# One-core transformer step on Trainium2: first modulation group loaded and multiplied in four parts, row vectors loaded later, overflow test moved before a wait

## The reference, cut to what matters

```
sh1, sc1, g1, sh2, sc2, g2 = split(silu(c) @ w_mod + b_mod, 6)      # w_mod: 1024 x 6144
h  = rmsnorm(x, norm1) * (1 + sc1) + sh1
p  = h @ w_in                                                       # 1024 x 1696, then three kinds of attention
x  = x + g1 * (heads_out @ w_out)
h2 = rmsnorm(x, norm2) * (1 + sc2) + sh2
x  = x + g2 * hier_moe(h2)                                          # 16 experts, each token goes to 2 of them
```

## Time and profile before

| | |
|---|---|
| median of three runs | 1391.71 us (1390.19 to 1394.88) |
| the profiled execution's own time | 1388.07 us |
| its span, first to last instruction | 1386.1 us |
| mean granted TensorE clock in it | 0.956 of full speed |
| PE busy | 1250.2 us, 90% |
| DVE, ACT, POOL busy | 539.7 us (39%), 377.7 us (27%), 156.2 us (11%) |
| DMA moved | 313.85 MB, mean 226 GB/s |
| SP's queue (q1), POOL's queue (q0), ACT's queue (q10) | 239.46, 47.20, 26.22 MB |

### The profile page before, as it was taken

One profiled execution on the slowest core, in us unless ns is written; L12 is line 12 of the kernel. 1 busy time (PEld: TensorE's weight loads), 2 busy tenths in 40 slices (PEclk: granted clock), 3 DMA queues, 4 the chain that ended last, 5 costly groups with the idle time before them and its releaser, 6 DMA issues.

```text
span 1386.1 us, 16841 instructions
## 1 busy us (share of the span) xinstructions
PE 1250.2 (90%) x5876; PEld 720.3 (52%) x5876; DVE 539.7 (39%) x1391; ACT 377.7 (27%) x963; POOL 156.2 (11%) x259
## 2 busy tenths in 40 slices
PE   3999989899999999999789997989999999999970
PEld 2455555565566554444355554556556655444430
DVE  0213256445565441121143324654546544111117
ACT  0112256434333111111012114653533311111111
POOL 3201120000000120000132003000000012000005
PEclk9999989998999999999989998999899999999995
DMA  9987577499111599999863047332001149999946
GB/s 336 393 293 253 199 278 268 147 360 331 41 61 62 203 336 384 359 373 365 299 239 105 22 167 265 123 123 68 32 31 62 61 191 333 397 369 368 366 167 227
DMA packets 125453, 313.85 MB, mean 226 GB/s; under 512 B 9841, under 2 KB 58257, under 8 KB 112705
## 3 DMA queue, kind: packets, MB, share of 16 engines
q1 hardware_dynamic: 90192, 239.46, 47.5%
q0 software_dynamic: 13136, 47.20, 9.1%
q10 hardware_dynamic: 22048, 26.22, 5.4%
HBM read 232.14 MB, written 80.71 MB: 226 GB/s over the span
## 4 chain that ended last, share of the span: by engine, by line
PE 81%; DVE 8%; issue 4%; ACT 3%; DMA 2%; POOL 1%; SPq 0%; DVEq 0%; ACTq 0%; POOLq 0%
PE ps L740 17%; PE ps L817 16%; PE ps L666 10%; PE ps L470 9%; PE ps L837 8%; PE ps L531 8%; PE ps L552 3%; PE ps L488 3%; DVE arena L1642 2%; PE ps L763 2%; PE ps L475 1%; DMA big<-in_x 1%; PE ps L606 1%; PE ps L517 1%; PE ps L781 1%
## 5 line engine op out<-in xcount | busy, mean ns | idle before, releaser
L740 PE MATMUL ps<-ring,big 128*128 128x384 f32 (+2 forms) x640 | 232.3, 522 | 3.9 <-ACT big L1196 3.9
L740 PEld LDWEIGHTS ps<-ring,big 128*128 128x128 f32 x640 | 121.0, 191 | 107.2 <-issue 64.7
L817 PE MATMUL ps<-ring,arena 128*128 128x512 f32 x384 | 169.3, 594 | 2.2 <-ACT arena L1289 2.0
L531 PE MATMUL ps<-arena 64*128 64x128 f32 (+5 forms) x576 | 143.4, 452 | 20.6 <-DVEq L1644 13.5
L470 PE MATMUL ps<-consts,arena 128*128 128x128 f32 (+2 forms) x872 | 130.2, 281 | 17.4 <-ACT arena L1112 6.2
L470 PEld LDWEIGHTS ps<-consts,arena 128*128 128x128 f32 (+2 forms) x872 | 103.7, 144 | 81.2 <-issue 53.6
L666 PE MATMUL ps<-ring,big 128*128 128x512 f32 x320 | 143.0, 598 | 0.9
L1112 ACT ACTIVATE arena<-ps 128x384 f32<-128x384 f32 (+3 forms) x140 | 69.0, 493 | 224.2 <-PE ps L470 223.7
L531 PEld LDWEIGHTS ps<-arena 64*128 64x128 f32 (+1 forms) x576 | 82.3, 208 | 80.8 <-issue 69.0
L817 PEld LDWEIGHTS ps<-ring,arena 128*128 128x128 f32 x384 | 71.2, 190 | 83.4 <-issue 83.4
L666 PEld LDWEIGHTS ps<-ring,big 128*128 128x128 f32 x320 | 59.0, 190 | 70.5 <-issue 66.4
(11 more groups left out here) (204 smaller groups left out, 1389.6 us busy)
## 6 DMA issues: line engine op xcount, KB each, us to landing
ring<-in_w_mod SPq DMA_DIRECT2D x40, 1024.0 KB, 10.6
ring<-in_w_up SPq DMA_DIRECT2D x22, 1024.0 KB, 9.3
ring<-in_w_gate SPq DMA_DIRECT2D x22, 1024.0 KB, 7.7
slots<-zeros ACTq DMA_DIRECT2D x8, 2560.0 KB, 18.7
slots<-zeros SPq DMA_DIRECT2D x8, 2560.0 KB, 20.3
arena<-in_w_down SPq DMA_DIRECT2D x16, 1024.0 KB, 13.0
slots<-arena POOLq DMA_DIRECT2D x32, 512.0 KB, 9.4
arena<-slots SPq DMA_DIRECT2D x30, 512.0 KB, 6.0
```

What stands on the lines that cost most here:

```text
L531: mm = pe.matmul(two(2 * h)[:, at:at + hi - lo], queries(pr, h), keys(pr, h, lo, hi), start=(at % 512 == 0), stop=True, skip_group_check=True)
L740: mm = pe.matmul(ps[:, c, 0:CHUNKS[c][1]], hT[:, s, k, :], slot[c][:, k, 0:CHUNKS[c][1]], start=(k == 0), stop=(k == KD - 1))
L817: mm = pe.matmul(ps[:, b, :], xgT[:, b, k * P:(k + 1) * P], w_gu[q][:, :, k, :], start=(k == 0), stop=(k == KD - 1))
```

## The change

1. *Norm weights in `consts`.* `n1c` and `n2c` become the columns behind the identity in `consts`. Their loads and semaphores go. `consts` comes in two loads: the first `HEAD` = 160 columns (identity and norm weights, 80 KB, semaphore `head_in`) and the rest (`const_in`).
2. *Group 0 in four parts.* Sixteen loads of 512 KB in place of eight of 1024 KB, with a semaphore for each pair of slices `k`. The order on SP's queue is now: part 0, tile 0's rows, part 1, the head of `consts`, part 2, part 3, chunk 0, tile 1, chunks 1 to 3, the rest of `consts`, tiles 2 to 4. PE multiplies a part when it is there; `turn_entry(0, 0)` comes after part 2; `spin(3, 6)` stands behind each of the parts 0, 1 and 2, in place of one `spin(3, 16)`; a `spin(3, 5)` stands behind `mod_columns(0)`.
3. *`cc` on ACT's queue* in place of SP's.
4. *`zero_fill` on ACT* one step later, at `s` = 1 to 4.
5. *`vector_loads(0)`* is issued by POOL after `entry(0, 1)` and the wait for the lane M, in front of the cache loads.
6. *DVE's wait for `const_in`* stands in front of the first rotary step and not at the start.
7. *Overflow test.* The load of the count and the branch come before the wait for the last stores; inside the branch the wait is repeated.

```diff
@@ tensor engine
-                    pe.wait_ge(mod0_in[ks[0] // 4], 64)
+                    pe.wait_ge(mod0_in[ks[0] // 2], 64)
...
-            mod_group(0, 0, range(0, 4))
-            pe.wait_ge(const_in, 16)
-            turn_entry(0, 0)
-            spin(3, 16)
-            mod_group(0, 0, range(4, 8))
+            for quarter in range(4):
+                mod_group(0, 0, range(2 * quarter, 2 * quarter + 2))
+                if quarter == 2:
+                    pe.wait_ge(head_in, 16)
+                    turn_entry(0, 0)
+                if quarter < 3:
+                    spin(3, 6)
             mod_columns(0)
+            spin(3, 5)
@@ sync engine
-            sp.dma_start(cc[:, 0, :], ...).then_inc(c_in, 16)
-            sp.dma_start(cc[:, 1, :], ...).then_inc(c_in, 16)
...
-            for half in range(2):
-                ks = slice(4 * half, 4 * half + 4)
+            for quarter in range(4):
+                ks = slice(2 * quarter, 2 * quarter + 2)
                 for i in range(4):
-                    sp.dma_start(slot0[i][:, ks, :], w_mod[:, ks, i * 512:(i + 1) * 512]).then_inc(mod0_in[half], 16)
-                if half == 0:
-                    sp.dma_start(consts[:, :], t_in["consts"]).then_inc(const_in, 16)
-                    sp.dma_start(n1c[:, :, :], t_in["norm1"]).then_inc(n1_in, 16)
-                    sp.dma_start(n2c[:, :, :], t_in["norm2c"]).then_inc(n2_in, 16)
+                    sp.dma_start(slot0[i][:, ks, :], w_mod[:, ks, i * 512:(i + 1) * 512]).then_inc(mod0_in[quarter], 16)
+                if quarter == 0:
                     x_load(t_in["x0"], 0)
+                if quarter == 1:
+                    sp.dma_start(consts[:, 0:HEAD], t_in["consts"][:, 0:HEAD]).then_inc(head_in, 16)
             in_load(0, 0)
             x_load(t_in["x0"], 1)
             in_load(0, 1)
             in_load(0, 2)
             in_load(0, 3)
+            sp.dma_start(consts[:, HEAD:], t_in["consts"][:, HEAD:]).then_inc(const_in, 16)
@@ scalar engine
+            act.dma_start(cc[:, 0, :], ...).then_inc(c_in, 16)
+            act.dma_start(cc[:, 1, :], ...).then_inc(c_in, 16)
...
-                        if s < 4:
-                            zero_fill(act, 2 * s, 2 * s + 2)
+                        if 1 <= s < 5:
+                            zero_fill(act, 2 * s - 2, 2 * s)
@@ gpsimd
-            vector_loads(0)
...
                 if L == 0:
                     pool.wait_ge(M.full, M[("mc", 0)])
+                    vector_loads(0)
...
-                for j in range(2):
-                    pool.wait_ge(ys_out[j], 16 * (E0 + NE) // 2)
                 pool.wait_ge(ctl_done, L + 1)
                 n_ov = pool.value_load(ctl[0:1, 0:1], min_val=0, max_val=NOVF)
                 with pool.If(n_ov > 0):
+                    for j in range(2):
+                        pool.wait_ge(ys_out[j], 16 * (E0 + NE) // 2)
...
+                for j in range(2):
+                    pool.wait_ge(ys_out[j], 16 * (E0 + NE) // 2)
@@ vector engine
-                dve.wait_ge(n1_in, 16)
+                dve.wait_ge(head_in, 16)
...
-            dve.wait_ge(const_in, 16)
...
                         if ORDER[i] != 4:
                             t = ORDER[i]
+                            dve.wait_ge(const_in, 16)
@@ tables
+HEAD = P + 2 * DEPTH * KD
-CONSTS = [("ident", P), ("upper", P), ("madd", 64), ("swa", 7 * P),
+CONSTS = [("ident", P), ("n1", DEPTH * KD), ("n2", DEPTH * KD), ("upper", P), ("madd", 64), ("swa", 7 * P),
```

More of the change, by code:

```diff
@@ L171, in program @@
         ident, upper = (cst[n] for n in ("ident", "upper"))
+        n1c, n2c = (cst[n].rearrange("p (l k) -> p l k", l=DEPTH) for n in ("n1", "n2"))
         ones = cst["w4"][:, 3:4].broadcast_to([P, P])
@@ L315, in program @@
         met = sem("met")
-        const_in, c_in, bmod_in, small_in, vec_in, nrm_in = (sem(n) for n in
-                                                    ("const_in", "c_in", "bmod_in", "small_in", "vec_in", "nrm_in"))
+        head_in, const_in, c_in, bmod_in, small_in, vec_in, nrm_in = (sem(n) for n in
+                                                    ("head_in", "const_in", "c_in", "bmod_in", "small_in", "vec_in", "nrm_in"))
         slot_in = [sem(f"slot{i}_in") for i in range(4)]
-        mods_done, mc_done, n1_in, n2_in, g2_in = (sem(n) for n in ("mods_done", "mc_done", "n1_in", "n2_in", "g2_in"))
-        mod0_in = [sem(f"mod0_in{i}") for i in range(2)]
+        mods_done, mc_done, g2_in = (sem(n) for n in ("mods_done", "mc_done", "g2_in"))
+        mod0_in = [sem(f"mod0_in{i}") for i in range(4)]
         mod_in = [sem(f"mod_in{i}") for i in range(2)]
@@ L1162, in beside @@
                         cp.then_inc(lane.free, 1)
+            act.dma_start(cc[:, 0, :], t_in["c"].rearrange("a (p k) -> (a p) k", k=KD)).then_inc(c_in, 16)
+            act.dma_start(cc[:, 1, :], t_in["c_ctx"].rearrange("(p k) -> p k", k=KD)).then_inc(c_in, 16)
             act.wait_ge(c_in, 32)
@@ L1548, in mod_columns2 @@
                 else:
-                    dve.wait_ge(n2_in, 16)
                     STT(modc2[:, :, 1, :], modc2[:, :, 1, :], 1.0, n2c[:, L:L + 1, :].broadcast_to([P, 2, KD]), ALU.add,
@@ L2055, in constants @@
     c = {
-        "ident": np.eye(P), "upper": query < key,
+        "ident": np.eye(P), "n1": norm1.reshape(DEPTH, KD, P).transpose(2, 0, 1), "n2": norm2.reshape(DEPTH, KD, P).transpose(2, 0, 1),
+        "upper": query < key,
         "madd": np.where(ok, 0, far),
@@ L2105 @@
     flat = {
-        "consts": constants(), "near": (np.arange(P) - FAR).astype(np.float32),
+        "consts": constants(x["norm1"], x["norm2"]), "near": (np.arange(P) - FAR).astype(np.float32),
         "x0": np.concatenate([x["x_sample"][0], x["x_prompt"][0]], 0),
         "c": x["c"], "c_ctx": x["c_ctx"], "w_mod": x["w_mod"], "b_mod": x["b_mod"],
-        "norm1": x["norm1"].reshape(DEPTH, KD, P).transpose(2, 0, 1), "norm2": x["norm2"],
-        "norm2c": x["norm2"].reshape(DEPTH, KD, P).transpose(2, 0, 1), "norm_final": x["norm_final"],
+        "norm2": x["norm2"], "norm_final": x["norm_final"],
         "w_in": w_in, "g_qa": x["g_qa"], "w_uq": x["w_uq"], "g_kva": x["g_kva"], "w_ukv": w_ukv,
```

6 lines of the change are left out of this document (1 added, 5 removed).

## The result

The changed kernel takes 1380.95 us (median of 6 runs, 1378.31 to 1385.58), the kernel before 1391.81 beside it (6 runs): a ratio of 0.9924, 95% interval 0.9902 to 0.9945. Forecast were 1379.3 and faster; the range of 1374 to 1386 holds the result. The gain is 10.9 us here. Run again on another chip the changed kernel took 1379.94 against 1387.86, ratio 0.9939 (0.9924 to 0.9953), a gain of 7.9 us.

A forecast was written before the change was run, and what follows sets the result against it. The kernel was taken as a line of PE work (PE busy 90% of the span), winnable only where it waits. Terms 9.1 + 1.7 - 1.0 + 2.6 = 12.4 us, off 1391.7, gave 1379.3 us, range 1374 to 1386.

The forecast's parts named there:

- (a): Head: with `cc` on ACT's queue, the first weight load is issued 0.9 us earlier.
- (b): Head: moving the spread norm row loads behind the modulation columns removes a stall of the modulation weights' stream, 3.2 us.
- (c): Head: taking most of `consts` from in front of the last modulation weights wins 3.0 us; norm loads counted as nothing.
- (d): Head: the last of four parts takes 1.8 us instead of 3.64, so modulation matmuls end 9.1 us earlier.
- (f): Clock term at the in-projection's start: 1.7 us won, bounds 0 to 1.7.
- The first rival: Head: waits for parts bring half clock, 1.7 us lost per fall; total 1382.7 to 1384.4 us. Chance 0.12.
- (g): In-projection: chunk 2 lands late behind row and cache loads; 1.0 us of new PE wait, between 0 and 2.3.
- The rival of an in-projection that outruns its weights: In-projection: row and cache loads put the load stream 4 to 5 us further behind; total 1384 us. Chance 0.12.
- (h): DVE's moved waits at `vec_in` and for the rest of `consts`: some 3 us of work behind `vec_in`, all hidden.
- (i): Zero fills one step later: a pair overlaps modulation group 1's loads, at half share 4 us, hidden by 1 us or more.
- rival 3: Head: each added load brings its own gap, 6 x 1.6 = 9.6 us given back; total 1388.9 us. Chance 0.06.
- Layer ends: Both layer ends: count and branch moved into the wait for the last store win 1.4 and 1.2 us, together 2.6.

The follow-up runs named there:

- e3: Changed kernel with the three spread row loads back behind the bias rows on POOL's queue, at about 10 us; 1382.75 us, ratio to the kernel before 0.9955.
- e4: Changed kernel with the rest of `consts` (1130 KB) issued right behind its head, before modulation parts 2 and 3; 1385.34 us, ratio to the kernel before 0.9978.
- e5: Changed kernel with modulation group 0 in two parts of 1024 KB loads and one spin of 16 between them; 1382.41 us, ratio to the kernel before 0.9938.
- e6: Changed kernel without the five spins behind the modulation columns; 1378.30 us (4 runs), ratio to the kernel before 0.9903.
- e12: Changed kernel with group 0 in five parts, overflow test before the last two experts' stores, 11 spins for 16 at layer 1's entry; 1375.18 us, ratio to before 0.9900.
- e7: Changed kernel with ACT's zero fills back at steps 0 to 3; 1381.49 us in one run.
- e10: Changed kernel with modulation group 0 in eight parts (32 loads of 256 KB), five spins before the last part; 1382.34 us, ratio to the kernel before 0.9935.
- e2: Kernel before with only the overflow test moved in front of the wait for the last stores; 1387.16 us against 1388.47, ratio 0.9995.
- e9: Changed kernel with the overflow test before the stores of the last two experts, stores in both arms; 1380.35 us, ratio to the kernel before 0.9922.
- e1: Changed kernel with the overflow test put back behind the wait for the last stores, head edits kept; 1381.22 us, ratio to the kernel before 0.9955.

## Why the prediction was right, step by step

The sign and the mechanism of the head were right; the mechanism at the layer ends was right for the instructions moved and wrong for the landing. The sum, 12.4 us, is too large: the profiled executions are 7.7 us apart, the medians on the second chip 7.9. On the first chip they are 10.9 apart, because the profiled execution of the kernel before lay 3.7 us below its median and that of the changed kernel 0.5. So the forecast of 1379.3 came within 2 us partly by luck. Of the prediction's own signs two went against it: the gathers start 0.86 and 0.83 us after the landings and not within 0.7, and from layer 1's in-projection on the stage borders come 7.7 to 6.4 us earlier, under the 8 us that it had set as the mark of being wrong.

(a) *Start of the stream.* SP's first issue is 0.9 us earlier, but the first 1024 KB only 0.5. Mis-sized by 0.4.

(b) *Row loads.* 3.2 us for the stall. Read off the landings of the kernel before it was right there (18.8 against 15.4), but it isn't a price of its own: put back into the new order, the same loads cost 1.35 (e3). The term stood for the whole interplay of what was in flight; what makes it 3 us in one order and 1.4 in the other was not tested. The landing of the last modulation weights moved by 6.4 us, from 33.98 to 27.55. Of these (a) has 0.5, `consts` 2.7 and the rows 1.35; about 1.9 belong to no single edit that was tried.

(c) *`consts`.* 3.0 forecast, 2.7 measured (e4). Right. The norm loads, taken at nothing, landed at 21.95 and 22.14 before, together 0.4 us behind `consts` (21.76), and are a small gain that was left out.

So the last modulation weights land at 27.55, forecast 26.9.

(d) *Four parts.* Forecast 1.8; two parts are 2.2 later (e5). The spins end at 27.7, within 0.1 us of the last landing, where the working had them end at 27.0: the 5.5 us from part 2's landing on were right, and that landing was at 22.1 and not at 21.5. The lead at the last modulation matmul is 8.4 us, 9.1 forecast: the difference is the landing.

(e) The way down to the in-projection is 3.8 us as before, and the five spins lie inside it.

(f) *Clock.* 1.7 forecast, which is 5 x 0.27 + 5 x 0.07, what the clock column of the earlier trace rows lacks of 1.00 (the runs give the clock as a share of full speed and never in GHz); 1.7 measured, and e6 shows that it goes when the last five spins go: 0.90 and 0.75 in its windows from 30 to 40, one stretch of 3.4 us at half clock. The first rival (clock lost between parts) did not come about: from part 1 on the parts take 1.92 or 1.93 us for 16 records, with 0.61 us of idle before part 2 and less before parts 1 and 3. Part 0, with nothing on PE before it, took 3.64, hidden by the wait for part 2.

(g) *What is late next.* 1.0 us of new wait forecast, none measured: chunk 2 landed at 44.9 and PE came at 45.1. The rows and caches held it for some 1.6 us (chunk 1 landed at 37.8, and 2048 KB are 5.4) and not for 3.4. It was right as a bound, only 0.2 us from biting; it bites in e12 (1.1 us) and e7 (1.5 us). The rival of an in-projection that outruns its weights is therefore the true next limit.

(h) *DVE.* Past `vec_in` at 42.2, before its first copy was due. Hidden as forecast; the slower rival had no ground.

(i) *Zero fills.* The shift keeps 1.5 us of wait off chunk 2 (e7), which the prediction had put into (g) without a number. No load stands among PE's waits from 160 to 330 us, before or after, so the other end is hidden too.

*Loads that bring their own gap (rival 3).* Eight loads more cost 0.3 us (e5), sixteen 0.3 to 0.4 (e10): 0.02 to 0.04 us each, not the 1.6 that a 4 KB load alone took. They were issued by SP into a stream that moved 390 GB/s from 25 to 30 us; the 4 KB load was issued at 1.3 us in the kernel before, which moved 15 GB/s from 1.2 to 3 us.

*Layer ends.* 1.4 and 1.2 forecast, 1.3 and 1.1 measured (rows of the chain, e2). This step was right in what it costed and wrong in its sum: the landing itself, taken as fixed at nearly 3 us, became 5.16 and 3.21. The term of 2.6 us came out at about nothing in the profiled execution, and it is the step of the prediction that failed. The 0.3 at layer 1 goes with an 8 KB packet of q14 in the flight (1341.2 us; e9 has none there and lands in 2.90); that q14 serves POOL is inferred: it starts 2.7 us behind the issue in all ten profiles that have it there, and leaves the flight when POOL's order changes (e1, e9). The 2.2 at layer 0 go with a 16 KB packet of the instruction queue q8, and e6 and e12 moved that packet by edits of PE's work (e12 also of POOL's order, which alone does not move it, e9), e12 back to a landing of 2.92. That q8 serves PE is inferred: it leaves the flight when PE's program gets 28 records shorter (e12), moves to its end with 20 fewer (e6), and stays in it when only POOL's, SP's or ACT's changes (e3, e4, e7, e9). In the trace of the changed kernel 258 records of PE (matmuls, weight loads and its sequencer) lie between two packets of q8 on average, with a spread of 16%, while the time between two packets spreads by 40% and the records of DVE and ACT by over 30% (41 intervals of 11 to 46 us, without the two over 100 us long among the experts). That the packet holds one of the 16 engines for over a microsecond and the store's share behind it is read from the packets' times: 128 packets of 4 KB, spread evenly, are 8 for each of the 16 engines, and two to eight of them start at its end, never more. The packet was not varied alone.

*Rest.* 1.2 us were lost in layer 1's body, where the changed kernel's profile has 3.4 us more at half clock than the one before. That goes either way from run to run: over the six runs of the changed kernel the fastest (1378.3 us) has a mean granted clock of 0.958, the slowest (1385.6) 0.950. The carry of 3.6 us from the profiled execution to the median, on which 1379.3 rests, is most likely of this kind; that was not shown.

## What to carry to other kernels

Where a program waits for its first weights, count the bytes that stand in front of them in the queue (here 1130 KB were 2.7 us), and split only the last piece, since the work behind the last landing is what counted (32 records in place of 16 behind it were 1.7 us); then see at once which load is wanted next, for it was 0.2 us from being the bound. Keep PE busy in the last short wait before a long run of matmuls: five useless matmuls in 2.3 us of idle were worth 1.7 us at that place, though not in the time of the whole kernel. When a test is taken off the path behind a store, look at what the store's flight then shares the DMA engines with (here one packet of 8 KB went with 0.3 us), and measure the landing and not only the instruction that moved.

## What the runs showed of the hardware that I had not expected

The packets of the instruction queues hold up the data's: in eleven flights two to eight of the store's 4 KB packets started at the end of q8's packet. One such packet of 16 KB took 1.0 to 2.1 us, and the 512 KB store with it landed in 4.6 to 5.3 us in place of 2.9. Its place went with the number of PE's records ahead of it: with 3006 matmul records ahead of layer 0's end it missed the flight, with 3016 to 3020 it fell into it. So an edit of the first 30 us changed a landing at 680 us by 2.2 us, and the next edit moved the same cost to 1335 us.

Reading a value into a register ahead of a branch cost POOL 0.8 to 0.95 us between a landing and the next DMA, and the branch itself 0.2 to 0.5.

The time at half clock ahead of the last layer end, added up over a profile, lay between 72 and 92 us in fourteen profiles of nearly the same program: worth up to 10 us (an estimate, half of that difference) that no edit here explains, more than most of the steps above. The fastest of these profiles (e9, 1374.22 us) has the 72, the slowest with the new head (e4, 1387.34) the 92.
